# A two-block network in one kernel: the gate rank of its linear attention computed in fp32 on four column groups of TensorE, with three small moves beside it

## The reference

```python
def first_block(x, ...):
    x = x + 0.5 * swiglu(rmsnorm(x, norm_ffn1_g), ffn1_w_gu, ffn1_w_down)
    x = x + hybrid_mixer(rmsnorm(x, norm_mix_g), w_in, conv_w, gate_w_up, gate_b, ...)
    x = x + 0.5 * swiglu(rmsnorm(x, norm_ffn2_g), ffn2_w_gu, ffn2_w_down)
    return rmsnorm(x, final_norm_g)

def hybrid_mixer(h, w_in, ...):
    z = h @ w_in                       # 1024 -> cb, cc, cu, q, k, v, g_lr, r, ga, gb
    ...                                # g_lr has GATE_RANK = 16 columns, v has 1024
    log_a = log_sigmoid(g_lr @ gate_w_up + gate_b) / 16.0     # 16 -> 512
    o = gla_chunked(q, k, v, log_a)    # chunks of 64 tokens, 4 heads
    ...
```

## Time and profile before

| | us |
|---|---|
| median of 3 runs | 1836.78 |
| lowest and highest | 1836.70, 1836.86 |
| the profiled execution | 1836.6 |
| its span, first to last instruction | 1834.8 |
| PE busy | 1825.8 (100%) |
| DVE busy | 966.5 (53%) |
| ACT busy | 623.7 (34%) |
| DMA read from HBM | 170.86 MB, 94 GB/s over the span |

### The profile page before, as it was taken

How to read it: one execution, slowest core, us unless ns; L and a number is a source line. 1 busy time by engine, 2 the same in 40 slices (tenths; PEclk the granted TensorE clock), 3 DMA queues, 4 the chain that set the end, 5 groups by cost and what they waited for, 6 DMA issues and landing times.

```text
span 1834.8 us, 20367 instructions
## 1 busy us (share of the span) xinstructions
PE 1825.8 (100%) x8372; PEld 1504.9 (82%) x8372; DVE 966.5 (53%) x1276; ACT 623.7 (34%) x891; POOL 37.7 (2%) x37
## 2 busy tenths in 40 slices
PE   9999999999999999999999999999999999999998
PEld 7888888878888888888888888888877788888887
DVE  6434434537775534546544443455687564535354
ACT  6222313434332323323432222234655432222133
POOL 0000000000000000000000000000133000000000
PEclk9999999999999999999999999999999999999999
DMA  5333332332122332232333223223521223232332
GB/s 175 104 94 99 95 103 87 96 107 81 58 81 94 102 103 92 94 101 92 96 100 99 97 92 104 92 81 121 149 70 59 81 92 104 92 103 92 103 92 69
DMA packets 52268, 176.38 MB, mean 96 GB/s; under 512 B 6448, under 2 KB 7600, under 8 KB 52176
## 3 DMA queue, kind: packets, MB, share of 16 engines
q1 hardware_dynamic: 50448, 171.99, 29.8%
q10 hardware_dynamic: 1312, 1.91, 0.3%
q0 software_dynamic: 416, 1.18, 0.3%
HBM read 170.86 MB, written 2.10 MB: 94 GB/s over the span
## 4 chain that ended last, share of the span: by engine, by line
PE 97%; DVE 1%; ACT 0%; DMA 0%; SPq 0%; issue 0%; DVEq 0%; ACTq 0%
PE ps L1422 29%; PE ps L1424 29%; PE ps L1423 29%; PE ps L1442 2%; PE ps L1444 2%; PE ps L1443 2%; PE ps L1733 0%; PE ps L1744 0%; PE ps L1758 0%; PE ps L1604 0%; DMA raw<-in_w_gu 0%; PE ps L1452 0%; PE ps L1607 0%; PE ps L1592 0%; DVE SS L800 0%
## 5 line engine op out<-in xcount | busy, mean ns | idle before, releaser
L1422 PE MATMUL ps<-Hhi,wh 128*128 128x512 f32 x1528 | 602.0, 394 | 0.0
L1423 PE MATMUL ps<-Hlo,wh 128*128 128x512 f32 x1528 | 594.9, 389 | 0.0
L1424 PE MATMUL ps<-Hhi,wl 128*128 128x512 f32 x1528 | 594.8, 389 | 0.0
L788 DVE TENSOR_TENSOR wl<-raw,wh 128x1024 fp32r<-128x1024 f32 (+1 forms) x319 | 387.6, 1216 | 130.4 <-ACT wh L382 128.6
L382 ACT ACTIVATE wh<-raw 128x1024 fp32r<-128x1024 f32 (+1 forms) x319 | 331.4, 1039 | 321.3 <-PE ps L1424 301.5
L1422 PEld LDWEIGHTS ps<-Hhi,wh 128*128 128x128 f32 x1528 | 286.9, 188 | 65.2 <-issue 4.9
L1423 PEld LDWEIGHTS ps<-Hlo,wh 128*128 128x128 f32 x1528 | 286.9, 188 | 60.9 <-issue 2.4
L1424 PEld LDWEIGHTS ps<-Hhi,wl 128*128 128x128 f32 x1528 | 286.8, 188 | 60.2
L1422 PE MATMUL ps<-Ahi,wh 128*128 128x512 f32 x792 | 308.3, 389 | 0.9 <-DVE Alo L1261 0.6
L1424 PE MATMUL ps<-Ahi,wl 128*128 128x512 f32 x792 | 308.1, 389 | 0.0
L1423 PE MATMUL ps<-Alo,wh 128*128 128x512 f32 x792 | 308.1, 389 | 0.0
(11 more groups left out here) (265 smaller groups left out, 1226.7 us busy)
## 6 DMA issues: line engine op xcount, KB each, us to landing
raw<-in_w_gu SPq DMA_DIRECT2D x86, 512.0 KB, 3.3
raw<-in_w_d SPq DMA_DIRECT2D x32, 512.0 KB, 3.6
raw<-in_w_up SPq DMA_DIRECT2D x32, 512.0 KB, 3.4
raw<-in_w_dn SPq DMA_DIRECT2D x32, 512.0 KB, 3.9
raw<-in_w_d SPq DMA_DIRECT2D x16, 384.0 KB, 3.1
raw<-in_w_v SPq DMA_DIRECT2D x8, 512.0 KB, 3.9
raw<-in_w_cc SPq DMA_DIRECT2D x8, 512.0 KB, 3.5
raw<-in_w_cu SPq DMA_DIRECT2D x8, 512.0 KB, 3.3
```

Source lines behind the costliest of these rows:

```text
L788: dve.tensor_tensor(WL[u % 3][:, 0:n], RAW[u % 3][:, 0:n], f32(WH[u % 3][:, 0:n]), ALU.subtract).then_inc(s["wl"], 1)
L1422: pe.matmul(ps, wh[:, c], hi[:, k, :], start=(k == 0), stop=False)
L1423: pe.matmul(ps, wh[:, c], lo[:, k, :], start=False, stop=False)
L1424: last = pe.matmul(ps, wl[:, c], hi[:, k, :], start=False, stop=(k == nb - 1))
```

## The change

Four edits:

1. The gate rank. g_lr is computed from X itself in plain fp32. Its weights, padded to 32 columns, are loaded as 128 KB; DVE multiplies them by the norm's gain into KST (two operations), ACT does nothing for that unit. PE runs eight fp32 matmuls of 128 × 32 against 512 tokens; feature tile k goes to column group k % 4 of the array, so partitions 32j to 32j + 31 of the bank hold the sum over the tiles j and j + 4. It stands inside the first unit of v, ahead of its fourth token block, and waits for the last Hlo tile.
2. The gate weights are repeated. gate_w_up, with 16 zero rows under it, stands four times under itself (128 rows, 256 KB); the gate's matmul contracts all 128 rows, and so also adds up the four groups.
3. ACT issues the first weights ahead of vec.
4. The first sums stand behind unit 2 and no longer in its middle.

With 1, v's first unit follows the feed-forward part directly, and its matmuls wait per feature tile for Hlo.

```diff
 def blocks(u):
+    if name == "w_glr":
+        return 2
@@ ACT, hi(u)
-            if u >= NU:
+            if u >= NU or u == U0["glr"]:
                 return
@@ ACT, start
+        act.dma_start(RAWS[:, 0:2, 0:256], dr["w_first"][0]).then_inc(s["fd0"], 16)
         act.dma_start(vec[:, :], dr["vec"]).then_inc(s["vec"], 16)
-        act.dma_start(RAWS[:, 0:2, 0:256], dr["w_first"][0]).then_inc(s["fd0"], 16)
@@ ACT, after the feed-forward part
-        act.dma_start(KR[0:16, 2, :], dr["gup"]).then_inc(s["mixc"], 16)
+        act.dma_start(KR[:, 2, :], dr["gup"]).then_inc(s["mixc"], 16)
@@ DVE, lo(u)
+            if u == U0["glr"]:
+                dve.wait_ge(s[f"raw{u % 3}"], 16 * (u // 3 + (u % 3 == 2)))
+                for i, done in enumerate(("wh", "wl")):
+                    w, g = (t[:, 128 * i:128 * i + 128].rearrange("p (k n) -> p k n", k=4) for t in (RAW[u % 3], KST))
+                    dve.tensor_tensor(g, w, vc("gm", 4 * i, 4).unsqueeze(2).broadcast_to([P, 4, 32]),
+                                      ALU.mult).then_inc(s[done], 1)
+                return
@@ DVE, first half of v
-                dve.tensor_tensor(KR[0:16, 3, :], BK[BANK[u]][0:16, :], R[0:16, :], ALU.mult).then_inc(s["ev"], 1)
+                dve.tensor_tensor(KR[:, 3, :], BK[BANK[u]][:, :], R[:, :], ALU.mult).then_inc(s["ev"], 1)
@@ PE, wide
-        def wide(name, half, free, steps):
+        def wide(name, half, free, steps, between=None):
                     if kk == 0:
                         free(t)
+                    if kk == 0 and t == 3 and between:
+                        between()
-                        if name == "nv":
-                            pe.wait_ge(s["hl"], 24 + k + 1)
+                        if name in ("v", "nv"):
+                            pe.wait_ge(s["hl"], (8 if name == "v" else 24) + k + 1)
@@ PE, ffn
-                        unit(u, Hhi, Hlo, mid=first_sums)
+                        unit(u, Hhi, Hlo)
+                        pe.wait_ge(s["ss"], 7)
+                        rows_sum(SS[:, :])
                         unit(u + 1, Hhi, Hlo)
@@ PE
+        def gate_rank():
+            u = U0["glr"]
+            pe.wait_ge(s["ev"], EVN[PREV[u]])
+            pe.wait_ge(s["hl"], 16)
+            for step in range(2):
+                for j in range(4):
+                    k = 4 * step + j
+                    last = pe.matmul(BK[BANK[u]][32 * j:32 * j + 32, :], KST[:, 32 * k:32 * k + 32], X[:, k, :],
+                                     start=(step == 0), stop=(step == 1))
+            last.then_inc(s["pe"], 1)
@@ PE, gate(h)
-            pe.matmul(BK[7][:, :], KR[0:16, 2, h * P:h * P + P], KR[0:16, 3, :], start=True,
+            pe.matmul(BK[7][:, :], KR[:, 2, h * P:h * P + P], KR[:, 3, :], start=True,
@@ PE, main order
-        unit(U0["glr"], Hhi, Hlo, "hl", 8)
-        wide("v", 0, mix_free, mix_steps)
+        wide("v", 0, mix_free, mix_steps, gate_rank)
@@ layout of the inputs
+            m["w_glr"] = np.ascontiguousarray(part.reshape(1, KT, P, 32).transpose(0, 2, 1, 3))
+    m["gup"] = np.ascontiguousarray(np.tile(np.concatenate([gup, np.zeros_like(gup)]), (4, 1)))
```

More of the change, by code:

```diff
@@ L1473, in first_units @@
                         last.then_inc(s["pe"], 1)
-        def first_sums():
-            pe.wait_ge(s["ss"], 7)
-            rows_sum(SS[:, :])
         def ffn(f, ready):
@@ L1948, in _layout @@
         if name == "glr":
-            part = np.concatenate([part, np.zeros((D, P - n), f)], axis=1)
-        m["w_" + name] = _wide(part) if name == "v" else _tiles(part)
+            part = np.concatenate([part, np.zeros((D, 32 - n), f)], axis=1)
+            m["w_glr"] = np.ascontiguousarray(part.reshape(1, KT, P, 32).transpose(0, 2, 1, 3))
+        else:
+            m["w_" + name] = _wide(part) if name == "v" else _tiles(part)
     m["w_oc"] = _tiles(a["w_out_conv"][0])
@@ L1962, in _layout @@
     m["w_dn"] = _tiles(a["w_down_2"][0])
-    m["gup"] = np.ascontiguousarray(a["gate_w_up"][0])
+    gup = a["gate_w_up"][0]
+    m["gup"] = np.ascontiguousarray(np.tile(np.concatenate([gup, np.zeros_like(gup)]), (4, 1)))
     fwd, bwd = a["ret_decay_fwd_2"][0], a["ret_decay_bwd_2"][0]
```

## The result

| | before | after |
|---|---|---|
| median, us | 1836.86 (7 runs) | 1830.76 (7 runs) |
| lowest and highest | 1836.66, 1837.38 | 1830.47, 1830.98 |
| the profiled execution | 1836.6 | 1830.98 |
| its span | 1834.8 | 1829.2 |

The ratio is 0.9966, with an interval of 0.9955 to 0.9978, so the kernel is faster, by 0.34%. The forecast was 1831.0, between 1829.9 and 1833.3. The profiled execution of the changed kernel is the longest of its seven, and that of the kernel before, 1836.6, is shorter than all the seven timed here, so the medians lie further apart than the profiles.

A forecast was written before the change was run, and what follows sets the result against it. PE was taken as the bound, busy 1825.8 of 1834.8 us. The terms −5.44 + 2.10 + 0.45 − 1.52 − 1.15 − 0.25 = −5.81 gave 1831.0 from the median 1836.78, range 1829.9 to 1833.3.

The forecast's parts named there:

- the four rivals: Alternatives to the forecast: groups not four at a time (0.17), no overlap (0.06), a passage per group change (0.05), late start (0.10).
- the in-order one: Gate rank: each matmul's second record holds back the next group, nine staggered steps, 4.13 us, time 1833.0; chance 0.09.
- Two at a time: Gate rank: only two column groups run at once, costing 3.81 us, time 1832.7; chance 0.08.
- no overlap: Gate rank: column groups don't overlap at all, 16 records one after another, 7.25 us, time 1836.1; chance 0.06.
- a passage at every change of group: Gate rank: each change of column group enters and leaves the split array again, 9.84 us, time 1838.7; chance 0.05.
- The wait at v: Start of the value projection: PE arrives 5.44 us earlier and waits for its low-order weights, +0.45, bounded by 0 and 0.6.
- The waits called met: Value projection and gate rank: output bank, last Hlo tile and third unit's weights are ready before PE needs them; cost nothing.
- The slide of the mean: Behind the first sums: PE delivers the mean's sum later, so row factor R and DVE's first rounds slide about 0.2.
- The cover at the seventh unit: Feed-forward part: seventh unit's weights ready about 39.4, PE asks at 39.9; thinnest cover, 0.5, beyond which delays cost time.
- The swap: Kernel start: first weights issued ahead of vec let PE start earlier, −0.25 us, range −0.5 to +0.3.
- the prediction's own second case: Kernel start: if ACT starts at 5.2, Hhi is there at 5.95 and only the second step gains, about 0.1.
- The rival that the start pays: Kernel start: vec comes late and the seventh unit's cover breaks; +0.55 or a few tenths, time about 1831.5; chance 0.10.

## Why the prediction was right

**The bound.** PE was the bound and stayed it. All of the 5.6 to 6.1 us came out of PE's own queue.

**The gate rank.** Predicted 2.10, measured 2.06. This was the uncertain term, and it decided. Four steps of 0.43 and one passage is what the trace shows, and one, two and four groups fit the same formula. Three of the four rivals fall with it, the in-order one among them. Two at a time (3.81) and in-order starts (4.13) are excluded by the changed kernel's own row; no overlap (7.25) describes the one-group run instead, at 7.17; a passage at every change of group (9.84) is excluded also by the group-by-group run, where changing the order of the groups cost nothing. The reading that carried it was that of L1733 and L1758: paired starts, not staggered ones, and one passage for eight matmuls that change group each time. That four groups would do what two do was an extrapolation, and the prediction called it one.

**The wait at v.** Predicted 0.45, measured 0.46, released by DVE as said. That it is a wait of its own and not a part of the passage is shown by the run with the weights earlier, where it is gone. The 0.03 for the signal rested on no row; here DVE ends at 366.80 and PE starts at 366.85. The waits called met (the bank, the last Hlo tile, v's third unit) didn't appear. How much the order matters there is seen with the gate rank in front: +2.10.

**The gates.** Predicted 0.38 each, measured 0.39, and put back by the run with 16 rows.

**The first sums.** Predicted −1.15, measured 2.01 − 0.86 = 1.15. The slide of the mean was 0.31, not 0.2, since PE arrived at 22.87 and not at 22.75, and DVE then waits for the signal. The cover at the seventh unit was 0.57, not 0.5. Neither cost anything. No run took that cover away, so that it is the thinnest stays argued.

**The swap.** Predicted −0.25 out of a range of −0.5 to +0.3. Unit 2 starts 0.14 sooner in the profiled execution, but the vec-first run started sooner still, so that is no proof of a gain. This is the term that isn't borne out. It put most of the gain into PE's first matmul, and that doesn't come sooner with the swap (5.97 against 5.88 on the mean), since PE then waits for ACT, which starts at 4.94 to 5.43. That is the prediction's own second case, "if ACT starts at 5.2", with about 0.1. The prediction saw that the first pair of matmuls ran as at the lower clock, but not that the rise comes at another moment in each execution and moves the start by up to 0.4, more than the term. At a like rise the swap is worth 0.17 and 0.05, from few executions, so its size stays open. The rival that the start pays had the right mechanism, a late vec, and came once, but dearer than the 0.55 it was given, since the drop of the clock was not in that price. It moved one run, not the median.

**The sum.** −5.81 predicted, −5.77 found line by line, −5.62 between the profiled executions and −6.10 between the medians. The misses of the terms are small (0.04, 0.01, 0.04, and 0.11 at the start) and the agreement doesn't come from large ones that cancel. The forecast is 0.24 off the median, about what two sets of runs of one kernel differ by (1830.76 and 1830.54). No row accounts for the 0.3 by which the medians fell further than the sum; the starts of the unprofiled runs can't be seen.

## What to carry to other kernels

A narrow fp32 product with a long contraction is cheapest with its slices spread over column groups (here 2.06 in four groups, 7.17 in one), and the next matmul adds up the groups for nothing if its weights are repeated. A small matmul on part of the array inside a regular stream pays 0.3 to 0.4 us to go into the split and out again, so a few zero rows that fill the array are cheaper than a short contraction. And in the first microseconds read several executions before believing a tenth: there the landing times and the moment of the clock's rise move by more than an edit is worth. Compare executions whose clock rose at about the same moment.

## What the runs showed of the hardware

- Column groups of the array run independently of the program's order among them: with four records of one group queued ahead of the next group's first, all four groups started within 0.04 us, and the eight matmuls cost 2.07 us as before.
- Since the groups run at once although they read all 128 rows each, four moving fp32 streams of 512 columns were fed together without slowing each other: a step took 0.43 to 0.44 with four groups and 0.43 with one.
- The granted clock at the start of a launch rose at another moment in each execution of the same warm-up, its record beginning between 4.27 and 7.19 us. PE's first pair of matmuls took 0.57 or 0.58 us behind an early rise and 0.89 to 0.99 ahead of a late one.
- After PE had stood for 2.22 us at the start its granted clock was 0.50 for the stretch of 8 to 11 us, at 1.2 GHz, and back at 1.00 in the next: a landing that let ACT start 1.21 us later cost 2.42 at the first sum.
- A load of 56 KB issued at 1.43 behind one of 256 KB on the same queue let ACT start between 4.94 and 5.43 in eight executions, and at 6.46 in a ninth; issued ahead of it, at 0.75, it let ACT start at 4.25, 4.02 and 3.96.
